# Hybrid decoder step on one core: new order of the attention and linear units, inverse roots on GpSimd, residual additions on VectorE

## The chip, the core and the metric

One program runs on one core of a Trainium2 chip. The time is the device time of a whole execution in microseconds. Lower is better. The engines are TensorE (PE, with its weight loads PEld), VectorE (DVE), ScalarE (ACT), GpSimd (POOL) and the DMA queues, of which the one on SyncE (SP) brings the weights and the one on GpSimd brings the cache. Each engine works through its own list in order, and semaphores join the lists.

## The reference

The kernel computes one inference step of a two-layer trunk for a prompt of 512 tokens and 8 samples with a paged past of 4096 tokens. Layer 0 is differential attention beside gated linear attention, layer 1 a recurrent block, and each layer ends in an MLP. What the change touches is this:

```python
def rmsnorm(x, g):
    xf = x.astype(jnp.float32)
    y = xf * lax.rsqrt(jnp.mean(xf * xf, axis=-1, keepdims=True) + EPS)
    return (y * g.astype(jnp.float32)).astype(x.dtype)
...
    a_out = rmsnorm(attend(da_q, da_k, da_v), g_da) * (1.0 - lam_init)      # diff_probs = softmax(l1) - lam * softmax(l2)
...
    def step(S, inp):                                                       # a chunk of 16 tokens
        o = jnp.einsum('bchs,bshv->bchv', att, vc) + jnp.einsum('bchk,bhkv->bchv', qe, S)
        S = jnp.exp(b_last)[..., None] * S + jnp.einsum('bshk,bshv->bhkv', kd, vc)
...
    o = rmsnorm(o.astype(h.dtype), g_gla) * jax.nn.silu(g_og)
...
        yp = yp + rmsnorm(mp, g[1])                                         # and again behind the MLP, g[3]
```

## The kernel before

All activations lie in transposed tiles of 128 features by 520 tokens (512 of the prompt, 8 samples). Weights stream in chunks of 1 MB; ScalarE splits each into a high part and VectorE into a low part, and TensorE makes three products (line 1689). This fills the long stages at the start and behind 613 us.

Between lies the mixer of layer 0. It interleaves two kinds of work:

- **The cache of the samples.** 128 pieces of 1 MB (64 of K, 64 of V) pass through a ring of 6 buffers. GpSimd issues each load (line 672) when the piece 6 places ahead has been used. Of each K piece GpSimd multiplies one half (line 629) and VectorE the other (1225), and VectorE reduces both (1213 for GpSimd's half, 1227 for its own). The function `k_chunks` does one K piece: reduce GpSimd's half of the piece before, then its own half of this one. GpSimd's next product waits for that first reduction, since it writes the same tile. V pieces are multiplied on TensorE (1850) with weights that GpSimd copies into `PM` (642).
- **The prompt.** First 16 attention units (4 heads by 4 query blocks), whose length in keys is 128, 256, 384, 512 in turn. Per unit: scores (1837), bias and row maximum on VectorE (1381, 1384, `maxima`), exponentials on ScalarE (868, `exponents`), inverse sums (1410), two scaled identities `DG` on ScalarE (915, 916), transposed difference of both softmaxes on TensorE (1878, 1879), its copy `AT` (923), and the output (1890). Then 8 linear units (4 blocks of 128 tokens by 2 head pairs). Per unit: transpose and mask the keys (1907, `KDM` 951), scores (1913), 8 updates on TensorE in two halves of 4 (1923), the chain of 8 states on VectorE (1449, `ST`), output products (1937, 1946), a state update for one sample (1827 and 1370), and three K and three V pieces.

Each unit's output is normalised two steps later: clamp (1390, 1393), sum of squares (904, `NSQ`), root on ScalarE (906, `NRT`), reciprocal and overflow test on VectorE (1399, 1400, `NRS`), a scaled identity (890, `NDG`), a product (1865) and a copy back (896).

The residual stream `X` has 8 tiles. Four times a norm of `ACC` is added to it (`post`): VectorE scales two tiles into `TMP` (1193) and adds the even one (1196), GpSimd adds the odd one (679). In the first and third of these VectorE also makes `H_lo` (1186) between the pairs.

The order on each engine is written out by hand; no scheduler moves anything. The unit loops before, on ScalarE (lines 908 to 928) and on VectorE (1406 to 1420), begin so:

```python
            if u + 1 < len(UNITS):
                exponents(u + 1)
            act.wait_ge(rr_ready, u + 1)
            A(DG[:, 0], IDENT, ACT.Copy, scale=RR[:, u % 2, 0:1])
...
            if u + 1 < len(UNITS):
                maxima(u + 1)
            ve.wait_ge(ex_done, u + 1)
            V.reciprocal(RR[:, u % 2], SM[:, u % 2]).then_inc(rr_ready, 1)
```

## Time and profile before

| | us |
|---|---|
| median of 3 runs | 1708.78 (1707.37 to 1712.07) |
| the profiled execution | 1708.17 |
| its span, first to last instruction | 1706.4 |
| attention units with cache work | about 237 to 393 |
| linear units with cache work | about 408 to 590 |
| the four residual additions | 676, 1074, 1284 and 1681 to 1694 |

The page's slices (one tenth of busy share per digit, 42.7 us each) show what kind of stage each is: TensorE stands at 9 in the long products and between 4 and 7 in the ten slices from 213 us on, which hold the units; the granted clock stands between 5 and 8 tenths there. A stage's own limits are read from the chain of waits and from the busy times of a window.

### The profile page before, as it was taken

Reading aid. Unit: us, or ns where it says so; the run is one execution under the profiler, and the core shown is the slowest. Engines: PE = TensorE matmul, PEld = TensorE weight load, DVE = VectorE, ACT = ScalarE, POOL = GpSimd, SP = SyncE. Lnnn points to the kernel's source line nnn. Section 1 sums busy time; section 2 is a strip of 40 time slices with the busy share of each in tenths; the row PEclk is TensorE's granted clock in tenths of the full one; section 3 lists DMA queues with packets and bytes.
Section 4 is the critical chain, followed back from the end, with each engine's and each line's share of the span. In section 5 each row is a group of like instructions: output and inputs, shape, how many; then the busy total and the mean of one; then the engine's idle time right before and its main releaser. Section 6 shows DMA issues by size and latency. Waiting matters only on the chain.

```text
span 1706.4 us, 25826 instructions
## 1 busy us (share of the span) xinstructions
PE 1462.3 (86%) x11004; PEld 1303.1 (76%) x11004; DVE 923.4 (54%) x1164; ACT 554.8 (33%) x861; POOL 346.4 (20%) x238
## 2 busy tenths in 40 slices
PE   4999946666667777999999999699897999999994
PEld 3999813334323366899999999589886999999994
DVE  3498867665777443743434352767718434343533
ACT  3323346662333323322222122437333222121222
POOL 0176755553555200100000000100302000000001
PEclk8999968887566679999999999799999999999997
DMA  8377688786767832123322322022221222223211
GB/s 289 124 270 258 250 288 325 294 315 257 287 229 274 295 142 75 60 90 100 99 75 99 99 78 97 3 74 76 75 75 49 79 96 99 87 87 99 89 61 51
DMA packets 127892, 250.32 MB, mean 147 GB/s; under 512 B 5267, under 2 KB 108455, under 8 KB 111136
## 3 DMA queue, kind: packets, MB, share of 16 engines
q0 software_dynamic: 18432, 134.23, 20.9%
q1 hardware_dynamic: 101984, 105.00, 19.2%
q10 hardware_dynamic: 7368, 9.50, 1.8%
q8 instruction: 87, 1.43, 0.4%
q14 instruction: 21, 0.17, 0.0%
HBM read 241.04 MB, written 7.73 MB: 146 GB/s over the span
## 4 chain that ended last, share of the span: by engine, by line
PE 74%; DVE 13%; ACT 7%; POOL 2%; issue 2%; DMA 1%; ACTq 0%; POOLq 0%; DVEq 0%
PE PS L1689 60%; PE PS L1674 3%; PE PS L1850 2%; POOL PROD L629 2%; DVE TMP L1193 2%; DVE SC L1213 1%; DVE RS L1167 1%; ACT PR L868 1%; PE PS L1923 1%; PE PS L1865 1%; PE PS L1983 1%; PE PS L1890 1%; PE PS L1878 1%; DVE PR L1381 1%; DVE MX L1384 1%
## 5 line engine op out<-in xcount | busy, mean ns | idle before, releaser
L1689 PE MATMUL PS<-H_hi,W_hi 128*128 128x260 f32 x1936 | 397.7, 287 | 24.7 <-DVE H_lo L1163 13.2
L1689 PE MATMUL PS<-H_hi,W_lo 128*128 128x260 f32 x1936 | 393.8, 285 | 0.0
L1689 PE MATMUL PS<-H_lo,W_hi 128*128 128x260 f32 x1936 | 393.6, 285 | 0.0
L1689 PEld LDWEIGHTS PS<-H_hi,W_hi 128*128 128x128 f32 x1936 | 303.8, 191 | 29.3 <-issue 22.1
L1689 PEld LDWEIGHTS PS<-H_hi,W_lo 128*128 128x128 f32 x1936 | 302.7, 191 | 0.0
L1689 PEld LDWEIGHTS PS<-H_lo,W_hi 128*128 128x128 f32 x1936 | 302.4, 191 | 0.0
L1158 DVE TENSOR_TENSOR W_lo<-RAW,W_hi 128x2048 fp32r<-128x2048 f32 x94 | 217.4, 2312 | 130.3 <-ACT W_hi L754 129.6
L754 ACT ACTIVATE W_hi<-RAW 128x2048 fp32r<-128x2048 f32 x94 | 179.4, 1909 | 278.0 <-PE PS L1689 277.7
L679 POOL TENSOR_TENSOR X<-X,TMP 128x520 f32<-128x520 f32 x16 | 26.7, 1668 | 938.8 <-DVE TMP L1193 938.8
L1689 PE MATMUL PS<-U_hi,W_lo 128*128 128x260 f32 x1024 | 206.4, 283 | 0.0
L1689 PE MATMUL PS<-U_lo,W_hi 128*128 128x260 f32 x1024 | 206.0, 283 | 0.0
L1689 PE MATMUL PS<-U_hi,W_hi 128*128 128x260 f32 x1024 | 206.0, 282 | 0.0
L629 POOL TENSOR_TENSOR PROD<-KV,QB 128x1024 f32<-128x1024 f32 x64 | 152.1, 2376 | 193.5 <-DVE SC L1213 164.4
L1689 PEld LDWEIGHTS PS<-U_hi,W_hi 128*128 128x128 f32 x1024 | 157.9, 188 | 0.0
L1689 PEld LDWEIGHTS PS<-U_hi,W_lo 128*128 128x128 f32 x1024 | 157.9, 188 | 0.0
L1689 PEld LDWEIGHTS PS<-U_lo,W_hi 128*128 128x128 f32 x1024 | 157.4, 188 | 0.0
L1553 DVE TENSOR_TENSOR ACC<-ACC,PS 128x520 f32<-128x520 f32 x64 | 44.6, 697 | 200.3 <-PE PS L1689 200.3
L1017 ACT ACTIVATE UF<-SQ 128x520 f32<-128x520 f32 x64 | 40.8, 638 | 279.9 <-DVE SQ L1543 279.9
L1850 PE MATMUL PS<-KV,PM 128*32 128x512 f32 x512 | 89.0, 782 | 29.8 <-POOL PM L642 20.7
L1543 DVE SCALAR_TENSOR_TENSOR SQ<-PS,RS 128x520 f32<-128x520 f32 x64 | 44.8, 700 | 112.9 <-PE PS L1689 112.9
L1674 PE MATMUL PS<-SQ,ONES 128*128 128x260 f32 x256 | 74.8, 449 | 36.0 <-ACT SQ L776 36.0
L1674 PEld LDWEIGHTS PS<-SQ,ONES 128*128 128x128 f32 x256 | 53.2, 222 | 56.8 <-issue 28.7
(292 smaller groups left out, 1598.7 us busy)
## 6 DMA issues: line engine op xcount, KB each, us to landing
RAW<-in_w_up SPq DMA_DIRECT2D x32, 1024.0 KB
RAW<-in_w_down SPq DMA_DIRECT2D x32, 1024.0 KB
RAW<-in_w_in_even SPq DMA_DIRECT2D x13, 1024.0 KB
RAW<-in_w_in_odd SPq DMA_DIRECT2D x8, 1024.0 KB
RAW<-in_w_out_odd SPq DMA_DIRECT2D x5, 1024.0 KB
RAW<-in_w_out_even SPq DMA_DIRECT2D x4, 1024.0 KB
x_saved<-X ACTq DMA_DIRECT2D x1, 2080.0 KB, 6.4
X<-x_saved SPq DMA_DIRECT2D x1, 2080.0 KB, 10.0
```

Source lines behind the costliest of these rows:

```text
L629: nc.gpsimd.tensor_tensor(PROD[:, 1], KV[i % RING][:, 2:4, :], QB[:, None, b % 2, :].to_broadcast([P, 2, 512]), ALU.mult).then_inc(prod1_r ...
L679: nc.gpsimd.tensor_tensor(X[:, kt], X[:, kt], TMP[:, 1], ALU.add).then_inc(x_odd, 1)
L754: A(W_hi[:, ch.slot], RAW[:, ch.slot], ACT.Copy).then_inc(w_hi_ready, 1)
L868: t = A(PR[:, u % 2, c, 0:n], PR[:, u % 2, c, 0:n], ACT.Exp, bias=MX[:, u % 2, c:c + 1], accum_out=SM[:, u % 2, c:c + 1])
L1017: A(UF[:, i], RL[:, i], ACT.Square).then_inc(uf_ready, 1)
L1158: V.tensor_tensor(W_lo[:, ch.slot], RAW[:, ch.slot], W_hi[:, ch.slot].bitcast(F32), ALU.subtract).then_inc(w_lo_ready, 1)
L1193: t = V.scalar_tensor_tensor(TMP[:, q], ACC[:, kt + q], VEC[:, gain + kt + q:gain + kt + q + 1], RS[:, 1], ALU.mult, ALU.mult)
L1543: V.scalar_tensor_tensor(pair(RL[:, i]), banks(ch.par[i]), 0.0, pair(RS[:, 1]), ALU.max, ALU.mult).then_inc(banks_free[ch.par[i]], 1)
L1553: V.tensor_tensor(pair(ACC[:, m]), pair(ACC[:, m]), banks(ch.par[i]), ALU.add).then_inc(banks_free[ch.par[i]], 1)
L1674: t = MM_(PS[:, 4 + i, 0:HALF], ONES[:], SQ[:, kt % 2, half], start=kt == 0, stop=kt == KT - 1)
L1689: t = MM_(PS[:, 2 * ch.par[i] + j, 0:HALF], w[:, ch.slot, k, cols], x[:, k, half], start=k == 0 and n == 0, stop=k == KT - 1 and n == 2)
L1850: t = MM_(PS[32 * pos:32 * pos + 32, 4, :], PM[:, part % 2, at:at + 32], KV[i % RING][:, pos, :], start=n % 32 == 0, stop=n % 32 == 31)
```

## The change

Seven edits, all in hand-written order or in who does an operation:

1. Attention, ScalarE: `DG` of a unit comes ahead of the exponentials of the next, and the copy `AT` ahead of the squares, `NDG` and the decay powers.
2. Attention, VectorE: the inverse sums of a unit come ahead of the maxima of the next.
3. The root on ScalarE and the reciprocal on VectorE go. GpSimd computes mean plus epsilon (one `tensor_scalar`) and raises it to the power -0.5 (one `tensor_tensor`), for 1 or 2 numbers per partition; the tables put this behind certain V pieces or ahead of certain K products. The overflow test stays on VectorE.
4. Linear units, TensorE: the second half of the updates has space of its own (banks 0 to 2), so it follows the first half at once; the state values come ahead of the normalisation; the normalisation and its copy stand ahead of the outputs, and the outputs wait once for all 8 states.
5. Linear units, VectorE: the second K piece and the overflow test come behind the state chain instead of ahead.
6. Linear units, ScalarE: `silu` stands ahead of the copy of the normalised output instead of behind.
7. VectorE adds all 8 residual tiles; the zeroing of `ACC` stays on GpSimd.

```diff
@@ gpsimd
+        POWERS_BEFORE_K = {K_IN_UNITS: (14, 15), **{K_IN_UNITS + 3 * u + 2: (15 + u,) for u in range(1, 6)}}
+        POWER_BEHIND_V = {**{2 * u + 1: u - 1 for u in range(1, 15)}, 51: 21, 54: 22, 57: 23}
+        def power(u):
+            n = len(outputs(u))
+            po.wait_ge(squares_summed, u + 1)
+            nc.gpsimd.tensor_scalar(NRT[:, u % 2, 0:n], NSQ[:, u % 2, 0:n], 2.0 ** -9, EPS / 1024, ALU.mult, ALU.add).then_inc(power_base, 1)
+            po.wait_ge(power_base, u + 1)
+            if u >= 2:
+                po.wait_ge(nd_ready, outputs_done(u - 1))
+            nc.gpsimd.tensor_tensor(NRS[:, u % 2, 0:n], NRT[:, u % 2, 0:n], EPSC[:, 2:2 + n], ALU.pow).then_inc(root_done, 1)
...
-        def post_add(i):
-            for kt in range(1, KT, 2):
-                po.wait_ge(post_odd, 4 * i + kt // 2 + 1)
-                nc.gpsimd.tensor_tensor(X[:, kt], X[:, kt], TMP[:, 1], ALU.add).then_inc(x_odd, 1)
@@ scalar, attention units
-            if u + 1 < len(UNITS):
-                exponents(u + 1)
             act.wait_ge(rr_ready, u + 1)
             A(DG[:, 0], IDENT, ACT.Copy, scale=RR[:, u % 2, 0:1])
             A(DG[:, 1], IDENTL[:], ACT.Copy, scale=RR[:, u % 2, 1:2]).then_inc(dg_ready, 1)
+            if u + 1 < len(UNITS):
+                exponents(u + 1)
+            act.wait_ge(at_done, u + 1)
+            A(AT[:, 0:n], PS[:, 2, 0:n], ACT.Copy).then_inc(at_copied, 1)
...
@@ vector
-                ve.wait_ge(post_even, 4 * i + kt // 2 + 1)
-                V.tensor_tensor(X[:, kt], X[:, kt], TMP[:, 0], ALU.add).then_inc(x_even, 1)
+                for q in range(2):
+                    ve.wait_ge(post_scaled, 8 * i + kt + q + 1)
+                    V.tensor_tensor(X[:, kt + q], X[:, kt + q], TMP[:, q], ALU.add).then_inc(x_added, 1)
...
@@ tensor, linear units
+            if u:
+                pe.wait_ge(st_ready, 8 * u)
             for first in (0, 4):
-                if first or u:
-                    pe.wait_ge(st_ready, 8 * u + first)
+                if first:
+                    pe.wait_ge(attm_ready, 2 * u + 2)
                 for n in range(first, first + 4):
...
-            if u:
-                normalise(15 + u, 2)
             state_values(u)
+            pe.wait_ge(st_ready, 8 * u + 8)
             v_chunks(34 + 3 * u, 1)
+            if u:
+                normalise(15 + u)
+                pe.wait_ge(nev_done, outputs_done(16 + u))
```

How the instructions stand, in the program's own lists. A bracket names the semaphores that an instruction waits for. ScalarE in the attention unit of head 2, first query block, before (its next unit has 256 keys):

```order
L868 ACTIVATE PR,SM<-PR,MX 128x256 [waits nm_ready]
L868 ACTIVATE PR,SM<-PR,MX 128x256
L915 ACTIVATE DG<-CONST,RR 128x128 [waits rr_ready]
L916 ACTIVATE DG<-IDENTL,RR 128x128
L904 ACTIVATE SQJ,NSQ<-OTC 128x128 [waits clamped]
L906 ACT_TABLE_LOAD
L906 ACTIVATE NRT<-NSQ,EPSC 128x1 [waits act_step]
L890 ACTIVATE NDG<-CONST,NRS 128x128 [waits nr_ready]
L923 ACTIVATE AT<-PS 128x128 [waits at_done]
L896 ACTIVATE PJ<-PS,G_129 128x128 [waits nmm_done]
L927 ACTIVATE OT<-PS 128x128 [waits o_done]
L868 ACT_TABLE_LOAD
```

and now:

```order
L926 ACTIVATE DG<-CONST,RR 128x128 [waits rr_ready]
L927 ACTIVATE DG<-IDENTL,RR 128x128
L883 ACTIVATE PR,SM<-PR,MX 128x256 [waits nm_ready]
L883 ACTIVATE PR,SM<-PR,MX 128x256
L931 ACTIVATE AT<-PS 128x128 [waits at_done]
L918 ACTIVATE SQJ,NSQ<-OTC 128x128 [waits clamped]
L905 ACTIVATE NDG<-CONST,NRS 128x128 [waits nr_ready]
L911 ACTIVATE PJ<-PS,G_129 128x128 [waits nmm_done]
L940 ACTIVATE OT<-PS 128x128 [waits o_done]
```

`DG` has moved ahead of the exponentials `PR`, `AT` ahead of the squares, and of the two table loads of a unit and the root none is left.

GpSimd in the fourth linear unit (K products `PROD`, cache loads `DMA`, weights of V pieces `PM`), before:

```order
L629 TENSOR_TENSOR PROD<-KV_69,QB 128x1024 [waits prod1_used,kv_loaded0]
L642 COPY PM<-SC_79 128x16x8 [waits soft_done,v_used]
L672 DMA KV_70<-in_cache_v,CIDX 128x2048 [waits v_used]
L672 DMA KV_69<-in_cache_k,CIDX 128x2048 [waits prod1_ready,k_used]
L629 TENSOR_TENSOR PROD<-KV_69,QB 128x1024 [waits prod1_used,kv_loaded2]
L672 DMA KV_69<-in_cache_v,CIDX 128x2048 [waits v_used]
L672 DMA KV_69<-in_cache_k,CIDX 128x2048 [waits prod1_ready,k_used]
```

and now:

```order
L638 TENSOR_TENSOR PROD<-KV_69,QB 128x1024 [waits prod1_used,kv_loaded0]
L651 COPY PM<-SC_79 128x16x8 [waits soft_done,v_used]
L699 DMA KV_70<-in_cache_v,CIDX 128x2048 [waits v_used]
L699 DMA KV_69<-in_cache_k,CIDX 128x2048 [waits prod1_ready,k_used]
L662 TENSOR_SCALAR NRT<-NSQ 128x2 [waits squares_summed]
L666 TENSOR_TENSOR NRS<-NRT,EPSC 128x2 [waits nd_ready,power_base]
L638 TENSOR_TENSOR PROD<-KV_69,QB 128x1024 [waits prod1_used,kv_loaded2]
L699 DMA KV_69<-in_cache_v,CIDX 128x2048 [waits v_used]
L699 DMA KV_69<-in_cache_k,CIDX 128x2048 [waits prod1_ready,k_used]
```

The two instructions of the power stand behind the second K product of the unit and the two loads that follow it, ahead of the third.

VectorE in the same linear unit, before (`SC` and `PROD` are a K piece, `S_163` the state of a sample):

```order
L1441 COPY_PREDICATED ATTM<-CONST,PS 128x128 [waits go_done,att_done,dve_step]
L1441 COPY_PREDICATED ATTM<-CONST,PS 128x128 [waits go_done,att_done]
L1213 TENSOR_REDUCE SC_74<-PROD 128x2x8 [waits prod1_ready]
L1225 TENSOR_TENSOR PROD<-KV_69,PS 128x1024 [waits kv_loaded0]
L1227 TENSOR_REDUCE SC_74<-PROD 128x2x8 [waits k_used]
L1399 RECIPROCAL NRS<-NRT 128x2 [waits root_done,dve_step]
L1400 SCALAR_TENSOR_TENSOR NRS<-NSQ,NRS 128x2 [waits dve_step]
L1449 SCALAR_TENSOR_TENSOR ST<-ST,DECC,PS 128x128 [waits u_done]
L1449 SCALAR_TENSOR_TENSOR ST<-ST,DECC,PS 128x128 [waits st_ready] x3
L1449 SCALAR_TENSOR_TENSOR ST<-ST,DECC,PS 128x128 [waits u_done,st_ready]
L1449 SCALAR_TENSOR_TENSOR ST<-ST,DECC,PS 128x128 [waits st_ready] x3
L1370 SCALAR_TENSOR_TENSOR S_163<-PS,KSS,S_163 64x128 [waits gs_v_done,st_ready]
```

and now:

```order
L1456 COPY_PREDICATED ATTM<-CONST,PS 128x128 [waits go_done,att_done,dve_step]
L1456 COPY_PREDICATED ATTM<-CONST,PS 128x128 [waits go_done,att_done]
L1461 SCALAR_TENSOR_TENSOR ST<-ST,DECC,PS 128x128 [waits u_done]
L1461 SCALAR_TENSOR_TENSOR ST<-ST,DECC,PS 128x128 [waits st_ready] x3
L1461 SCALAR_TENSOR_TENSOR ST<-ST,DECC,PS 128x128 [waits u_done,st_ready]
L1461 SCALAR_TENSOR_TENSOR ST<-ST,DECC,PS 128x128 [waits st_ready] x3
L1229 TENSOR_REDUCE SC_74<-PROD 128x2x8 [waits prod1_ready,st_ready]
L1241 TENSOR_TENSOR PROD<-KV_69,PS 128x1024 [waits kv_loaded0]
L1243 TENSOR_REDUCE SC_74<-PROD 128x2x8 [waits k_used]
L1415 SCALAR_TENSOR_TENSOR NRS<-NSQ,NRS 128x2 [waits root_done,dve_step]
L1386 SCALAR_TENSOR_TENSOR S_163<-PS,KSS,S_163 64x128 [waits gs_v_done]
L1386 SCALAR_TENSOR_TENSOR S_163<-PS,KSS,S_163 64x128 x3
```

The second K piece has moved behind the 8 states; the overflow test `NRS` waits there for `root_done`, which GpSimd now gives, and the state of the sample and the third K piece stand behind it.

## Rows read from the trace of the kernel before

**Rows 1.** The page: the span.
```profile
span 1706.4 us, 25826 instructions
```

**Rows 2.** Windows of attention and linear units: length, busy us (instructions), clock, DMA.
```profile
237.00:393.00 156.00, 105.41 (x590) 53.27 (x590) 101.28 (x164) 94.39 (x229) 88.65 (x71) 0.85 0.82 310
408.00:590.00 182.00, 123.04 (x843) 60.61 (x847) 126.72 (x213) 59.01 (x169) 92.82 (x72) 0.63 0.70 261
```

**Rows 3.** TensorE's timeline, outputs of first and last attention unit: start, us.
```profile
243.53 0.49 PE L1890 MATMUL PS<-VT,AT 128*128 128x128 f32 x2
...
391.05 1.16 PE L1890 MATMUL PS<-VT,AT 128*128 128x128 f32 x8 [0.46 <-ACT PJ L896]
```

**Rows 4.** Chain of waits through one attention unit (512 keys next): start, us.
```profile
334.43 1.08 PE PS L1837 x4
...
338.05 1.52 ACT PR L868 x4
...
345.00 0.74 PE PS L1865 x2
...
345.77 0.38 ACT PJ L896
346.19 0.82 PE PS L1890 x5
```

**Rows 5.** ScalarE's groups: table loads at the root; count, busy us, mean ns.
```profile
L906 ACT ACT_TABLE_LOAD x20 | 25.7, 1283 | 0.3
```

**Rows 6.** VectorE's timeline in the same unit: overflow test and one K piece.
```profile
338.38 0.16 DVE L1400 SCALAR_TENSOR_TENSOR NRS<-NSQ,NRS 128x1 f32<-128x1 f32 x1
338.46 1.22 DVE L1213 TENSOR_REDUCE SC<-PROD 128x16 f32<-128x1024 f32 x1
339.58 1.21 DVE L1225 TENSOR_TENSOR PROD<-KV,PS 128x1024 f32<-128x1024 f32 x1
```

**Rows 7.** GpSimd's timeline: a K product, a load, a small copy.
```profile
339.82 2.36 POOL L629 TENSOR_TENSOR PROD<-KV,QB 128x1024 f32<-128x1024 f32 x1 [3.64 <-DVE SC L1213]
...
344.47 0.94 POOL L672 DMA_INDIRECT KV<-in_cache_k,CIDX  x1 [0.30 <-issue]
...
355.02 0.40 POOL L642 COPY PM<-SC 128x128 f32<-128x128 f32 x1
```

**Rows 8.** Window of the attention stage in which DMA is fullest.
```profile
360.00:370.00 10.00, 5.58 (x36) 2.79 (x37) 6.66 (x12) 7.79 (x21) 3.34 (x5) 0.99 0.99 408
```

**Rows 9.** Cache tiles in the attention stage, issue to landing.
```profile
DMA to landing us min/median/max: 5.2/8.0/10.6
```

**Rows 10.** VectorE's timeline in the fourth linear unit, from clamp to clamp.
```profile
481.89 0.42 DVE L1393 TENSOR_SCALAR OTC<-PS 128x256 f32<-128x256 f32 x1 [6.39 <-ACT OT L963]
...
493.78 1.50 DVE L1449 SCALAR_TENSOR_TENSOR ST<-ST,DECC,PS 128x128 f32<-128x128 f32 x4 [1.65 <-PE PS L1923]
497.78 1.45 DVE L1370 SCALAR_TENSOR_TENSOR S<-PS,KSS,S 64x128 f32<-64x128 f32 x4 [2.50 <-PE PS L1827]
...
504.22 0.41 DVE L1393 TENSOR_SCALAR OTC<-PS 128x256 f32<-128x256 f32 x1
```

**Rows 11.** TensorE's timeline: outputs of that unit, then the next unit's transpose.
```profile
499.47 0.80 PE L1937 MATMUL PS<-GVT,ATTM 128*128 128x128 f32 x2
...
502.98 0.47 PE L1907 MATMUL PS<-CONST,KD 128*128 128x128 f32 x1
```

**Rows 12.** Timeline of the second residual addition, VectorE and GpSimd.
```profile
1074.45 1.43 DVE L1193 SCALAR_TENSOR_TENSOR TMP<-ACC,VEC,RS 128x520 f32<-128x520 f32 x2
1075.80 0.69 DVE L1196 TENSOR_TENSOR X<-X,TMP 128x520 f32<-128x520 f32 x1
1075.96 1.67 POOL L679 TENSOR_TENSOR X<-X,TMP 128x520 f32<-128x520 f32 x1 [381.55 <-DVE TMP L1193]
...
1076.53 2.34 DVE L1193 SCALAR_TENSOR_TENSOR TMP<-ACC,VEC,RS 128x520 f32<-128x520 f32 x2
...
1079.51 2.34 DVE L1193 SCALAR_TENSOR_TENSOR TMP<-ACC,VEC,RS 128x520 f32<-128x520 f32 x2
```

More of the change, by code:

```diff
@@ L230, in trunk @@
     V_CONVW, V_CONVB, V_BA, V_BX, V_LAM = 64, 96, 104, 112, 120
-    EPSC = small("EPSC", 2)
+    EPSC = small("EPSC", 4)
     PTB = sb("PTB", [P, N_SAMPLE * N_PAGES], I32, r_1 + 33792)
@@ L533, in outputs_done, with update, norm_bank @@
         return u if u <= len(UNITS) else 2 * u - len(UNITS)
+    def update(n, rows):
+        bank, at = (3, n) if n < 4 else (n // 2 - 2, 2 + n % 2)
+        return PS[rows, bank, P * at:P * at + P]
+    def norm_bank(u, i):
+        return PS[:, 3, P:2 * P] if u < len(UNITS) else PS[:, i, 2 * P:3 * P]
     def state(tb, n):
@@ L643, in weights @@
                                   SC[b % SLOTS][:, :, 16 * half:16 * half + 16].rearrange("p j n -> p n j")).then_inc(pm_ready, 1)
+        K_IN_UNITS = sum(UNIT_STEPS) + 2 * 11 + sum(PRE_STEPS)
+        POWERS_BEFORE_K = {K_IN_UNITS: (14, 15), **{K_IN_UNITS + 3 * u + 2: (15 + u,) for u in range(1, 6)}}
[8 more added lines that the diff above has]
+            nc.gpsimd.tensor_tensor(NRS[:, u % 2, 0:n], NRT[:, u % 2, 0:n], EPSC[:, 2:2 + n], ALU.pow).then_inc(root_done, 1)
         def release(i):
@@ L657, in release @@
                 po.wait_ge(v_used, n + 1)
+                if n in POWER_BEHIND_V:
+                    power(POWER_BEHIND_V[n])
         AHEAD = 1
@@ L664, in _ @@
                     if j < LOADS and ORDER[j][0] == "k":
+                        for u in POWERS_BEFORE_K.get(ORDER[j][1], ()):
+                            power(u)
                         pool_product(ORDER[j][1])
@@ L901, in squares_of @@
             act.wait_ge(clamped, u + 1)
-            n = len(outputs(u))
             for i, (at, tile, cols) in enumerate(outputs(u)):
                 t = A(SQJ[:, at], OTC[:, at], ACT.Square, scale=2.0 ** -4, accum_out=NSQ[:, u % 2, i:i + 1])
-            link(t)
-            A(NRT[:, u % 2, 0:n], NSQ[:, u % 2, 0:n], ACT.Sqrt, scale=2.0 ** -9, bias=EPSC[:, 1:2]).then_inc(root_done, 1)
+            t.then_inc(squares_summed, 1)
         act.wait_ge(identl_ready, 1)
@@ L1398, in inverse_norm @@
             n = len(outputs(u))
-            link(V.reciprocal(NRS[:, u % 2, 0:n], NRT[:, u % 2, 0:n]))
             V.scalar_tensor_tensor(NRS[:, u % 2, 0:n], NSQ[:, u % 2, 0:n], SQUARE_OVERFLOWS ** 2 / 256, NRS[:, u % 2, 0:n],
@@ L1406, in _ @@
         for u in range(len(UNITS)):
+            ve.wait_ge(ex_done, u + 1)
+            V.reciprocal(RR[:, u % 2], SM[:, u % 2]).then_inc(rr_ready, 1)
             if u + 1 < len(UNITS):
                 maxima(u + 1)
-            ve.wait_ge(ex_done, u + 1)
-            V.reciprocal(RR[:, u % 2], SM[:, u % 2]).then_inc(rr_ready, 1)
             if u:
@@ L1859, in past_output, with normalise @@
             t.then_inc(ogt_done, 1)
-        def normalise(u, bank):
+        def normalise(u):
             for i, (at, tile, cols) in enumerate(outputs(u)):
                 pe.wait_ge(nd_ready, outputs_done(u) + i + 1)
-                MM_(PS[:, bank, P + P * i:2 * P + P * i], OT[:, at], NDG[:, at], start=True, stop=True).then_inc(nmm_done, 1)
+                MM_(norm_bank(u, i), OT[:, at], NDG[:, at], start=True, stop=True).then_inc(nmm_done, 1)
         scores(0)
```

77 lines of the change are left out of this document (32 added, 45 removed).

## The prediction

> **What bounds the kernel now.** I read the span first [rows 1], then the windows of the two loops of units, then the chain of waits through one unit, then what each engine does there. The profiled execution took 1708.17 us, 1.8 us more than its span, and lies 0.6 us under the median of the three runs, so a sum made against it holds for the median as well. TensorE is full outside the mixer. Inside it no engine is: in the attention stage TensorE is busy 105 of 156 us, VectorE 101, ScalarE 94, GpSimd 89, and DMA 82% [rows 2]. What sets the end there is a chain that goes round all of them. Row by row in the unit shown: scores 1.08, VectorE's bias and maxima, exponentials 1.52, `DG`, then the transposes, a V piece, the normalisation 0.74, its copy 0.38, the output, and only then the next scores [rows 4]. From the first unit's output to the last one's it is 391.05 - 243.53 = 147.5 us, 9.8 us for each of 15 units [rows 3]. The linear stage takes 182 us with VectorE busy 127 of them [rows 2]; one unit is 22.3 us from clamp to clamp, and VectorE waits for TensorE twice in it, 1.65 and 2.50 us [rows 10]. The four residual additions are short chains in which TensorE only sums.
>
> **Attention units (edits 1, 2 and 3).** `DG` of a unit no longer waits for the maxima and exponentials of the next, so TensorE's transposes and first V piece run beside them. The new loop through ScalarE is: scores, maxima, exponentials, `AT`, squares, `NDG`, normalisation, its copy, output. In the unit shown: 5.1 up to the exponentials [rows 4], about 0.5 + 0.5 + 0.4 for the three on ScalarE (the like of the copy there, 0.38, with hand-overs), 0.74 + 0.38, output 0.9: 8.5 us. By the same count the other three lengths give 7.1, 5.8 and 7.1 (the parts in front shrink with the keys), 7.1 in the mean. The table loads cost 1.28 us each [rows 5]; the program has 54 before and 17 now, 37 fewer or 47 us of ScalarE, but ScalarE wasn't full, and only those on this loop count; they are already out of it in the sum. The Trainium skill says in "ScalarE: Activation LUTs", section on table sets, that a change of set costs about 2.7 us and that work should be batched by set. The trace agrees with the batching and disagrees with the price, 1.28 against 2.7; by the page's figure the removed loads would be 100 us of ScalarE and not 47.
>
> Two other limits stand close to it. One is DMA: a unit brings 3 pieces, 3.15 MB, and the fullest window moved 408 GB/s at 99% [rows 8]: 7.7 us per unit. The other is new. GpSimd now does the power of a unit behind its second V piece, and VectorE waits for it ahead of its K piece, whose first reduction GpSimd's next product waits for. Round that loop: overflow test 0.16, reduction 1.22 [rows 6], hand-over 0.1, product 2.36, two loads with their gaps 2.5 [rows 7], 0.2 for the copy into `PM` that falls on every second unit, hand-overs 0.3, and the power: 6.9 us plus x.
>
> **The price of a power, x.** The trace shows no power. It is two dependent GpSimd instructions on 1 or 2 numbers per partition. The nearest row is the copy of 128 numbers per partition, 0.40 us; the farthest is the product of 1024 at 2.36 us [rows 7]. So a pair lies between 0.2 us (two instructions of half the small copy) and 4.7 us (two of the large). I take two small copies and a hand-over, 0.9 us, since one number is much nearer to 128 than to 1024. Then GpSimd's loop is 7.8 us. The Trainium skill's "GPSIMD Engine Reference", section on instruction dispatch, says that the first call of a freshly loaded GpSimd kernel costs about 6 us more; no row here shows such a call, and if a power needed one the sum would be about 6 us worse, once.
>
> With limits of 7.1, 7.7 and 7.8 us that don't peak in the same units, and with 0.5 to 1.5 us of preparation of the linear units on VectorE in eight of the units, I take 8.5 us. 15 x (9.8 - 8.5) = 20 us saved. The floor is 7.8 (30 saved), and the ceiling, if the cache pieces land late, is 9.8 (nothing). VectorE's reciprocal (0.15) is gone too, and hidden.
>
> At the hand-over to the linear units the powers 14 and 15 stand in GpSimd's list ahead of the first K product and behind two loads, and the copy and squares of unit 15 wait for the first of them. Before, VectorE had the root in hand at once. I charge 2.5 us (the two loads) on the path to the sample's state outputs.
>
> **Linear units (edits 3 to 6).** The two waits of 1.65 and 2.50 us go: the second half of the updates follows at once, and the state values are ready early. But the second K piece, which stood ahead of the states while TensorE worked, now stands behind them, and behind it VectorE waits for the power. GpSimd can start its product only when the first reduction of that K piece is done, then issues two loads, then does the power: 0.1 + 2.36 + 2.5 + 0.9 = 5.9 us later [rows 7], while VectorE needs only 2.4 for the rest of the K piece [rows 6]. It stands 3.4 us. Behind it are the state of the sample (1.45) and the third K piece on VectorE, and `NDG`, the product, its copy and the outputs (3.5 us [rows 11]) on the way to the clamp. From the end of the states: K piece 3.65, wait 3.4, test 0.2, then `NDG` 0.7, product 1.2, `silu` with its table load or the copy 1.3 to 1.9, outputs 3.5, copy and clamp 0.7 (the small ones by the like of rows 4, with hand-overs), together about 15; from the clamp to the end of the states 8.4 (V piece 1.9, two halves of updates 4.0, the rest). 23.5 us against 22.3 [rows 10]. The first unit, where the K piece filled a wait, loses 2.7; the middle five lose about 1 each, the last two nothing. I take +8 us, with bounds -10 (both old waits gained, no new one) and +20 (x of 2.5 us).
>
> The last normalisation now waits for a power that GpSimd does after a V piece is used, on the way to the output projection: x, the test, `NDG` and hand-overs, +2.2 us.
>
> **Residual additions (edit 7).** Before, each pair after the first has one scaling held up by GpSimd's addition: two scalings take 2.34 us where undisturbed they take 1.43, and from pair to pair it is 2.98 us [rows 12]. With GpSimd out and one more addition of 0.69 on VectorE a pair is 1.35 + 0.65 + 0.70 = 2.70. Three pairs save 0.8, and at the end VectorE's last addition is done 0.5 us earlier than GpSimd's. The two with `H_lo` come to 1.2 in the same way, since there one `H_lo` was held up. 4 x 1.25 = 5 us saved, all on the path, since TensorE waits for the sums.
>
> **Sum.** -20 + 2.5 + 8 + 2.2 - 5 = -12.3 us, 1708.2 - 12.3 = 1696 us.
>
> **Rivals.** (a) The linear units gain too. If GpSimd's loads and product run ahead so that the power waits for nobody, VectorE's two waits are simply gone: 8 units x 2.5 us or so less than I count, some 14 us. 1682 us. For it: GpSimd is idle half of this stage (93 of 182 us [rows 2]). Against it: the power's place behind the second product.
>
> (b) The attention units are held by the cache. The ring reaches two units ahead. Loads go out after the product, some 8 us into a unit, and land 8.0 us later at the median, 10.6 at most [rows 9]; two units of 8.5 leave only 1.5 us beyond the median. If DMA near its full rate lands later, the period settles at 9.3 us: 12 us less gain, 1708 us, no change.
>
> (c) Slower: the power is dear. GpSimd's two instructions at 1.2 us and more each hold 15 attention units (period 6.9 + x), 7 linear units and the two hand-overs. From x = 1.6 on each further microsecond costs 24. The sum reaches zero near x = 1.8; at x = 2.2 the time is 1717 us. For it: this operation is the only one here with no row. Against it: it has one number per partition.
>
> **Chances.** Forecast 0.42, with its own range 1688 to 1702; (a) 0.20; (b) 0.15; (c) 0.15; the remaining 0.08 is linear units that lose much more than I count, 1704 to 1712. One measurement tells about 0.3% from no change, 5 us, so faster means under 1703.6 and slower over 1713.9. Faster takes the forecast, (a) and a fifth of (b) and little more: 0.66. Same takes most of (b) and some of the rest: 0.14. Slower takes (c), a fifth of (b) and the worst of the rest: 0.20. The range 1677 to 1714 leaves out most of (c) and the best of (a).
>
> **What would show it.** In the profile after: period of the attention outputs (8.5 us); span between GpSimd's `NRT` and `NRS` starts and the next load (0.9 us); VectorE's idle time ahead of `NRS` in units 1 to 5 of the linear part (3.4 us, put down to GpSimd); clamp to clamp 23.5 us; pairs of additions 2.70 us. I am wrong if the attention period stays over 9.3 us, if the power pair takes over 1.6 us, or if VectorE doesn't wait ahead of the overflow test in the linear units.

## The result and the profile after

The changed kernel takes 1682.07 us (median of 4 runs, 1680.55 to 1683.37) against 1709.13 us: ratio 0.984, interval 0.9823 to 0.9857, 27 us faster. The forecast was 1696 us, 13 us faster. The sign and the range held; the size was about half of what came. The profiled execution of the changed kernel took 1682.64 us, and its page says

```profile
span 1680.8 us, 25820 instructions
```

which is 25.6 us less than [rows 1]. The windows of the two loops of units in the changed kernel (length, busy us of PE, PEld, DVE, ACT and POOL, clock, DMA share, GB/s) answer to [rows 2]:

```profile
242.00:364.00 122.00, 97.36 (x568) 46.92 (x560) 96.79 (x143) 54.72 (x184) 95.11 (x93) 0.86 0.95 365
386.00:565.00 179.00, 117.37 (x831) 59.54 (x831) 121.13 (x210) 44.09 (x148) 98.60 (x84) 0.64 0.71 258
```

From first to last output the attention stage is a sixth shorter with the same work: DMA went from 82% to 95%, ScalarE fell from 94 of 156 us to 55 of 122. TensorE's first and last attention outputs answer to [rows 3]:

```profile
242.42 0.49 PE L1904 MATMUL PS<-VT,AT 128*128 128x128 f32 x2
...
365.37 0.82 PE L1904 MATMUL PS<-VT,AT 128*128 128x128 f32 x5 [0.46 <-ACT PJ L911]
```

365.37 - 242.42 = 123.0 us, 8.2 us a unit instead of 9.8. Between such landmarks both executions can be laid side by side. OS is VectorE's first operation on the sample's state outputs. The clamps are those of [rows 10], one for each linear unit; the linear units are numbered 0 to 7, and "unit 3" is the time from the clamp of [rows 10] to the next. The output projection is its first product, line 1704 now.

| stretch | before | after | change | forecast |
|---|---|---|---|---|
| start to first attention output | 243.5 | 242.4 | -1.1 | |
| first to last attention output | 147.5 | 123.0 | -24.6 | -20 |
| last output to OS (hand-over) | 16.4 | 20.5 | +4.1 | +2.5 |
| OS to first clamp (linear unit 0) | 20.2 | 23.0 | +2.8 | +2.7 |
| first to eighth clamp | 158.0 | 155.8 | -2.2 | +5 |
| eighth clamp to output projection | 27.3 | 29.9 | +2.6 | +2.2 |
| the rest, with the four additions | 1093.4 | 1086.2 | -7.2 | -5 |

In linear unit 3 (clamp to clamp, VectorE; start, us, what, and in brackets the idle time ahead and its releaser) the rows answer to [rows 10]:

```profile
459.90 0.42 DVE L1409 TENSOR_SCALAR OTC<-PS 128x256 f32<-128x256 f32 x1 [6.84 <-ACT OT L977]
...
464.61 3.03 DVE L1461 SCALAR_TENSOR_TENSOR ST<-ST,DECC,PS 128x128 f32<-128x128 f32 x8 [0.25 <-PE PS L1939]
467.67 1.22 DVE L1229 TENSOR_REDUCE SC<-PROD 128x16 f32<-128x1024 f32 x1
468.81 1.21 DVE L1241 TENSOR_TENSOR PROD<-KV,PS 128x1024 f32<-128x1024 f32 x1
470.05 1.22 DVE L1243 TENSOR_REDUCE SC<-PROD 128x16 f32<-128x1024 f32 x1
475.33 0.16 DVE L1415 SCALAR_TENSOR_TENSOR NRS<-NSQ,NRS 128x2 f32<-128x2 f32 x1 [4.06 <-POOL NRS L666]
475.41 1.43 DVE L1386 SCALAR_TENSOR_TENSOR S<-PS,KSS,S 64x128 f32<-64x128 f32 x4
...
481.90 0.42 DVE L1409 TENSOR_SCALAR OTC<-PS 128x256 f32<-128x256 f32 x1
```

The two waits of [rows 10] are gone in this unit: the 8 states now run in one piece, and the sample's state waits no longer for TensorE. In their place stands 4.06 us for `NRS`, which GpSimd gives. GpSimd's timeline in the same unit shows what stood ahead of it:

```profile
469.04 2.36 POOL L638 TENSOR_TENSOR PROD<-KV,QB 128x1024 f32<-128x1024 f32 x1 [2.69 <-DVE SC L1229]
...
471.89 1.01 POOL L699 DMA_INDIRECT KV<-in_cache_v,CIDX  x1 [0.16 <-issue]
...
474.22 0.19 POOL L662 TENSOR_SCALAR NRT<-NSQ 128x2 f32<-128x2 f32 x1
474.50 0.72 POOL L666 TENSOR_TENSOR NRS<-NRT,EPSC 128x2 f32<-128x2 f32 x1
```

The product starts when VectorE has done the first reduction of the K piece behind the states. Then come the copy of the V weights, two loads and the power. The two instructions of a power take 0.19 + 0.72 us for two numbers per partition, 1.0 us from start to end, and 0.8 for one number. VectorE stands 3.7 to 4.6 us for the power in units 2 to 5, but only 1.15 us in unit 1 (at 423.00 us) and 2.2 us in unit 6.

### The profile page after: what moved, and what is told of

It reads as the page before. It is cut to its first block, busy times and chain, and to the rows that moved or that the text cites. A ratio compares the mean times of both kernels' runs of the same rounds, so it can differ in the third digit from the quotient of the medians.

```text
span 1680.8 us, 25820 instructions
## 1 busy us (share of the span) xinstructions
PE 1455.7 (87%) x11004; PEld 1298.4 (77%) x11004; DVE 913.1 (54%) x1157; ACT 500.1 (30%) x800; POOL 339.4 (20%) x270
## 3 DMA queue, kind: packets, MB, share of 16 engines
q8 instruction: 87, 1.43, 0.3%
## 4 chain that ended last, share of the span: by engine, by line
PE 74%; DVE 13%; ACT 4%; POOL 4%; issue 2%; DMA 2%; ACTq 0%; DVEq 0%; POOLq 0%
PE PS L1704 61%; PE PS L1689 3%; POOL PROD L638 3%; PE PS L1864 2%; DVE SC L1229 2%; DVE RS L1182 1%; PE PS L1939 1%; DVE TMP L1208 1%; PE PS L1996 1%; POOL KV L699 1%; DVE ST L1461 1%; DVE X L1212 1%; DVE ACC L1613 1%; PE PS L1959 1%; DMA out_gla_prompt<-ST 1%
## 5 line engine op out<-in xcount | busy, mean ns | idle before, releaser
L715 POOL TENSOR_TENSOR INP<-GX,ACC 128x520 f32<-128x520 f32 x7 | 14.5, 2079 | 505.9 <-ACT GX L1100 499.4
```

## The experiments

Each starts from the changed kernel unless it says otherwise. "Attention" is first to last attention output, "linear" OS to the eighth clamp, in the profiled execution.

| kernel | median us | ratio to before, interval | attention | hand-over | linear |
|---|---|---|---|---|---|
| before | 1707.6 to 1714.2 | | 147.5 | 16.4 | 178.2 |
| the changed kernel | 1682.07 | 0.984 [0.9823, 0.9857] | 123.0 | 20.5 | 178.8 |
| e1 linear power early | 1672.39 | 0.9789 [0.9767, 0.9811] | 123.1 | 19.3 | 169.6 |
| e2 linear root on ScalarE | 1670.37 | 0.9772 [0.9745, 0.98] | 122.9 | 19.2 | 169.3 |
| e3 attention order back | 1701.33 | 0.9958 [0.9939, 0.9977] | 144.5 | 18.2 | 180.9 |
| e4 additions back | 1690.5 | 0.9884 [0.986, 0.9908] | 123.4 | 20.4 | 181.5 |
| e5 attention root on ScalarE | 1708.91 | 0.9992 [0.9976, 1.0009] | 149.8 | 16.0 | 180.4 |
| e6 power longer | 1707.57 | 0.9984 [0.9968, 0.9999] | 132.5 | 22.7 | 192.2 |
| e7 e1 and copy early | 1662.82 | 0.9725 [0.9697, 0.9753] | 122.9 | 20.5 | 160.6 |
| e8 copy early alone | 1675.45 | 0.9788 [0.9759, 0.9817] | 124.1 | 20.4 | 174.2 |
| e9 half the bytes of V | 1684.41 | 0.9848 [0.981, 0.9885] | 123.0 | 19.2 | 179.9 |
| e10 all powers early | 1653.04 | 0.9673 [0.9641, 0.9705] | 124.2 | 15.3 | 158.1 |
| e11 e10, copies early everywhere | 1651.94 | 0.9663 [0.9629, 0.9698] | 123.2 | 17.1 | 154.1 |
| e12 K piece ahead | 1666.44 | 0.9752 [0.9722, 0.9781] | 123.4 | 19.3 | 161.0 |
| e13 e12, halves share space | 1675.65 | 0.9771 [0.9742, 0.98] | 123.6 | 20.8 | 179.1 |
| e14 silu behind | 1685.95 | 0.9835 [0.981, 0.9859] | 123.1 | 20.8 | 181.4 |
| e15 e11, K piece ahead | 1647.35 | 0.9622 [0.9594, 0.965] | 123.1 | 15.9 | 151.6 |
| e16 e15, linear root on ScalarE | 1654.86 | 0.9656 [0.9628, 0.9685] | 122.7 | 17.5 | 154.4 |

The kernel before was measured again beside each group of experiments, and its median moved between 1707.6 and 1714.2 us; where two groups are compared, the ratios are the better guide. The last three columns come from one execution each. Kernels that share the program of a stage show how far such a column wanders: 122.9 to 124.1 us in attention, 19.2 to 20.8 at the hand-over, and 178.8 to 181.5 in the linear units (the changed kernel, e3, e4, e5 and e9). A difference inside these bands says nothing.

**Attention: which edit?**

```diff
@@ e3: scalar (vector likewise: maxima(u + 1) ahead of the inverse sums)
+            if u + 1 < len(UNITS):
+                exponents(u + 1)
             act.wait_ge(rr_ready, u + 1)
             A(DG[:, 0], ...)                       # and AT again behind decay_powers
@@ e5: scalar, squares_of(u), u < 16 (e2 further down: the same for u >= 16)
+                link(t)
+                A(NRT[...], NSQ[...], ACT.Sqrt, ...).then_inc(root_done, 1)     # reciprocal on VectorE
```

> The changed kernel with ScalarE's and VectorE's order in the attention units put back (exponentials and maxima of the next unit ahead of the scaled identities and inverse sums, the copy AT behind the squares), the power kept on GpSimd. The attention outputs lie 8.2 us apart in the changed kernel and 9.8 us in the one before. Theory (the order made the gain, the root's table loads only little): period 9.3 us or more, time 1698 us or more. Rival (the 2 table loads of 1.28 us per unit that went made it): period 8.6 us or less, time under 1689 us.

> The changed kernel with the roots of the 16 attention units back on ScalarE (square root, reciprocal on VectorE), the new order kept; the linear units keep the power. Theory (the two edits need each other: in the new loop the squares stand between the copy AT and the normalisation, so a root puts its two table loads of 1.28 us on the loop through ScalarE, while in the old order they cost only 3 us in all): attention period 9.3 us or more against 8.2, time 1697 us or more. Rival (the order alone gives the gain, the cache's transfers hold the period near 8.2 us anyway): period 8.5 us or less, time under 1688 us.

The numbers of both theories came out (periods of 9.6 and 10.0 us). The reason that e3's theory gave, that the order alone made the gain, did not; e5's, that the edits need each other, did. With neither edit the stage takes 147.5 us, with the power alone 144.5, with the order alone 149.8, with both 123.0: the first is worth 3 us alone, the second nothing, together they are worth 24.6. TensorE's timeline of e3 (the transposes of two units in a row) shows why the power alone gives little: they still wait for `DG`, which stands behind the next unit's exponentials.

```profile
311.12 0.49 PE L1892 MATMUL PS<-DG,PR 128*128 128x128 f32 x2 [2.28 <-ACT DG L929]
...
321.23 0.49 PE L1892 MATMUL PS<-DG,PR 128*128 128x128 f32 x2 [2.33 <-ACT DG L929]
```

ScalarE's timeline of e5 shows why the order alone gives nothing: between `AT` and the normalised copy (at 317.07) stand the squares, the table load, the root, `NDG`, a second load, and the decay powers `KD`, the exponential that needs it.

```profile
312.01 0.60 ACT L942 ACTIVATE AT<-PS 128x512 f32<-128x512 f32 x1 [2.57 <-PE PS L1906]
...
312.91 1.28 ACT L928 ACT_TABLE_LOAD   x1
314.20 0.29 ACT L928 ACTIVATE NRT<-NSQ,EPSC 128x1 f32<-128x1 f32 x1
314.41 0.39 ACT L912 ACTIVATE NDG<-CONST,NRS 128x128 f32<-128x128 f32 x1
314.81 1.28 ACT L906 ACT_TABLE_LOAD   x1
316.10 1.06 ACT L906 ACTIVATE KD<-KD 128x1024 f32<-128x1024 f32 x1
```

**Attention: what holds the 8.2 us?**

```diff
@@ e9: gpsimd, loads
+                if kind == "v" and 6 <= n < 32:
+                    dst, src = dst[:, 0:1024], ...  # half a row
@@ e6: gpsimd, power(u)
+            for k in range(2):
+                po.wait_ge(power_base, 3 * u + 1 + k)
+                nc.gpsimd.tensor_tensor(NRX[:, 0:n], NRT[:, u % 2, 0:n], EPSC[:, 2:2 + n], ALU.pow).then_inc(power_base, 1)
```

> The changed kernel, but the loads of V pieces 6 to 31 (those of the attention units) bring only half of the bytes (half of each row, from other rows of the cache), so an attention unit brings 2.1 MB instead of 3.15 MB; GpSimd issues as many loads, and the output of the past's attention is not the reference's. Theory A (transfers set the 8.2 us between attention outputs, with DMA at 95% and 365 GB/s there): first to last attention output 117 us or less instead of 123.0, time 1677 us or less. Theory B (the loops through the engines, GpSimd's of 7.8 us and ScalarE's, set it): 121 us or more, time 1680 to 1683 us.

> The changed kernel with two more powers ahead of each power, into a spare tile, so that the pair of GpSimd instructions of 0.85 us becomes about 2.2 us long. Theory A (GpSimd's loop of K product, loads and power is the next limit in attention, at 7.8 us): period 9.0 to 9.2 us instead of 8.2, and with the linear units, the two hand-overs and the end 20 us or more: 1702 us or more. Theory B (the cache's transfers set the 8.2 us and the power stands beside them): period under 8.5 us, the rest of the program 6 to 10 us, time 1688 to 1693 us.

The transfers don't hold it. The window of the attention stage, of the changed kernel and then of e9:

```profile
237.00:365.00 128.00, 102.35 (x582) 48.58 (x582) 97.79 (x144) 55.06 (x186) 97.36 (x96) 0.85 0.92 354
```

```profile
237.00:365.00 128.00, 102.10 (x582) 50.42 (x582) 98.71 (x145) 54.91 (x185) 97.35 (x97) 0.85 0.73 255
```

354 GB/s become 255 and DMA falls from 92% to 73%, and the first and last attention outputs stay 123.0 us apart, as theory B said. (The median, 1684.41 us, lies 1.4 us over its range; the ratio is that of the changed kernel within the interval.) In e6 the pair is longer by 1.5 us in the linear units (GpSimd's timeline, the two extra powers and the real one):

```profile
495.53 1.49 POOL L666 TENSOR_TENSOR NRX<-NRT,EPSC 128x2 f32<-128x2 f32 x2
497.10 0.69 POOL L670 TENSOR_TENSOR NRS<-NRT,EPSC 128x2 f32<-128x2 f32 x1
```

and by 1.3 in attention. The attention stage grew by 9.5 us, 0.6 a unit, to a period of 8.8 us. Neither theory's period holds (9.0 to 9.2, or under 8.5), though theory A's time of 1702 us or more does. A reading that fits is that GpSimd's loop is the longest in part of the units only. The whole kernel lost 25.5 us, most of the rest (13.4) in the linear units. GpSimd's loop in the changed kernel reads

```profile
316.73 1.84 POOL L699 DMA_INDIRECT KV<-in_cache_v,CIDX  x1 [0.15 <-POOL PROD L638]
318.88 0.94 POOL L699 DMA_INDIRECT KV<-in_cache_k,CIDX  x1 [0.30 <-issue]
319.89 0.19 POOL L662 TENSOR_SCALAR NRT<-NSQ 128x1 f32<-128x1 f32 x1
320.16 0.56 POOL L666 TENSOR_TENSOR NRS<-NRT,EPSC 128x1 f32<-128x1 f32 x1
320.90 1.01 POOL L699 DMA_INDIRECT KV<-in_cache_v,CIDX  x1 [0.18 <-issue]
323.17 2.34 POOL L638 TENSOR_TENSOR PROD<-KV,QB 128x1024 f32<-128x1024 f32 x1 [1.26 <-DVE SC L1229]
325.68 1.85 POOL L699 DMA_INDIRECT KV<-in_cache_v,CIDX  x1 [0.16 <-POOL PROD L638]
```

Where GpSimd's loop holds a unit (it stands idle only 0.3 us ahead of its product), one turn is 7.1 us when both issues behind the product are short (products at 290.25 and 297.38), and 8.0 us when one of them takes 1.85 us, as in the rows above (products at 323.17 and 331.15; in e9 at 314.31, 322.28 and 330.25).

**The linear units: the power's place, and who stands beside it.**

```diff
@@ e1: gpsimd
-        ... **{K_IN_UNITS + 3 * u + 2: (15 + u,) for u in range(1, 6)}}
+        ... **{K_IN_UNITS + 3 * u + 1: (15 + u,) for u in range(1, 6)}}
@@ e7 (with e1), e8 (alone): gpsimd, ahead of the products of a step
+                if ORDER[i - RING][0] == "v" and ORDER[i - RING][1] >= 32:
+                    next_weights(ORDER[i - RING][1])          # the copy into PM
```

> The changed kernel with one edit: in linear units 1 to 5 the power stands ahead of the second K product instead of behind it and its two loads. In the changed kernel VectorE stands 3.7 to 4.6 us ahead of the overflow test in each of these units. Theory: this wait is on the path and nothing else is close behind it, so clamp to clamp of these five units falls from 22-25 us to 18-19 us and the time from 1682 to about 1663 us. Rival: another limit (the cache pieces' landing, TensorE's third V piece, GpSimd's own products) is right behind; then the wait goes but clamp to clamp stays over 20.5 us and the time over 1674 us.

> The changed kernel with the roots of the 8 linear units back on ScalarE (square root, reciprocal on VectorE), all orders kept. Theory (the power's place behind GpSimd's product costs the linear units 3.7 to 4.6 us each, and the root itself was never on the path there, since ScalarE idles 13 us in a unit): the wait of VectorE goes, its two table loads per unit are hidden, time 1660 to 1668 us. Rival (the root off ScalarE is what paid for the linear units): the table loads come on the path between the normalisation and the outputs, 1680 us or more.

> The first experiment (power of linear units 1 to 5 ahead of the second K product) and besides, in the linear units, the copy of the V weights (PM) ahead of the K product instead of behind it. In the first experiment units 3 and 4 fell from 22 to 18-20 us, unit 5 stayed at 25 us and unit 2 at 26.5, where a V piece waits for that copy. Theory (in these units a second chain of about the same length, product, copy, V piece, stands beside VectorE's wait for the power): unit 5 falls to 20-21 us, unit 2 by 2 to 3 us, time 1664 to 1667 us. Rival (something else holds these units): 1670 us or more.

> The changed kernel with only the copy of the V weights moved ahead of the K product in the linear units, the power where it is. Theory (two chains side by side, the wait for the power being the longer or equal): unit 5 stays within 1.5 us of 25, in all at most 4 us faster than the changed kernel, 1678 to 1682 us; the sum of this and of the first experiment's gain is smaller than the gain of both together. Rival (the copy was the limit and the power's wait beside it costs nothing): unit 5 at 21 us, time under 1677 us.

e1 lies between its two numbers. Its expectation says that VectorE waits 3.7 to 4.6 us in each of units 1 to 5; that holds for units 2 to 5. Units 3 and 4 fell from 22.0 and 22.4 us to 18.2 and 19.7, but unit 5 stayed at 25.1 and unit 2 at 26.5. VectorE's timeline of e1: in unit 4 the test waits for nothing; in unit 5 neither, but the sample's state behind it waits 4.38 us for TensorE.

```profile
485.91 0.16 DVE L1415 SCALAR_TENSOR_TENSOR NRS<-NSQ,NRS 128x2 f32<-128x2 f32 x1
...
506.34 0.16 DVE L1415 SCALAR_TENSOR_TENSOR NRS<-NSQ,NRS 128x2 f32<-128x2 f32 x1
510.88 1.45 DVE L1386 SCALAR_TENSOR_TENSOR S<-PS,KSS,S 64x128 f32<-64x128 f32 x4 [4.38 <-PE PS L1841]
...
518.63 0.42 DVE L1409 TENSOR_SCALAR OTC<-PS 128x256 f32<-128x256 f32 x1 [2.22 <-ACT OT L977]
```

The chain of waits there goes through GpSimd's product, the copy into `PM`, and the V piece that needs it:

```profile
504.07 2.35 POOL PROD L638
506.42 0.35 POOL PM L651
...
506.90 1.94 PE PS L1864 x8
508.84 2.00 PE PS L1841 x2
510.84 1.86 PE PS L1864 x8
```

e7 moves this copy ahead too, and unit 5 falls to 18.8 us: the time is 1662.8 us, just under the theory's range. e8, the copy alone, gave 6.6 us: its time lies on the rival's side, since unit 2 fell from 28.2 to 24.0, where the copy alone was last; unit 5 fell to 23.6, within the theory's 1.5 us. The gains are 9.7 and 6.6 us alone and 19.3 together (8.7, 8.9 and 19.7 by the ratios); the 2 to 3 us between sum and whole are no more than the intervals allow. Unit 5 is the clear sign of two chains side by side: 25.0 us, 25.1 with the power early, 23.6 with the copy early, 18.8 with both. e2, just outside its first range, takes the linear units to 169.3 us, as e1 does: they lose 9 us by the power's place.

**The linear units: the K piece, the two halves, silu.**

```diff
@@ e12: vector, linear units
             slot(GLA_SLOT + 2 * u)
+            k_chunks(min(max(steps - 1, 0), 1))
             for n in range(8):
...
-            k_chunks(min(max(steps - 1, 0), 1))
@@ e13 (with e12): tensor
+        return PS[rows, 3, P * (n % 4):P * (n % 4) + P]
+                if first or u:
+                    pe.wait_ge(st_ready, 8 * u + first)
@@ e14: scalar
             if u:
                 normalised(15 + u)
+            if 1 <= u <= 4:
+                A(PJ[:, 19 + u], PJ[:, 19 + u], ACT.Silu).then_inc(silu_ready, 1)
```

> The changed kernel with the second K piece of the linear units ahead of the 8 states on VectorE again, as in the kernel before; the overflow test stays behind the states. Theory (with the K piece behind, GpSimd's product starts late, and the power behind it is what VectorE and TensorE wait for; with it ahead the product runs beside the states): the wait for the power falls from 4 us to under 1.5 us, units 1 to 5 at 19 to 21 us, 1668 to 1674 us. Rival (the states come 3.7 us later and TensorE's outputs with them, which eats it): 1680 us or more.

> The experiment with the K piece ahead of the states, and in it the two halves of the updates share space again, so that the second half waits for the first 4 states (with the V piece between the halves, as before). Theory (this edit alone is what the linear units gain most by, since VectorE's wait between the two halves, 1.65 to 2.15 us in every unit before, is on the path in all 8 units): 1.5 to 2.5 us per unit given back, first clamp to last 152 to 158 us instead of 141.9, time 1677 to 1684 us. Rival (the gain comes from the outputs' and the state values' place instead): under 5 us in all, time under 1672 us.

> The changed kernel with silu behind the copies of the normalised output again on ScalarE (units 1 to 4). I had charged silu 1.3 to 1.9 us on the path of each unit in its new place; in the trace of the changed kernel it takes 0.62 us beside the product. Theory (silu is off the path in both places, no table load is left there): within 2 us of the changed kernel, 1680 to 1684 us. Rival (its place decides when the outputs start): 1685 us or more.

e12 is 15.6 us faster than the changed kernel, more than expected, though units 1 and 2 stay at 24.5 and 24.8 us. VectorE's timeline, unit 3: the K piece fills the time of the updates, GpSimd's product runs beside the states, and the wait for the power is 1.73 us instead of 4.06 (under 1.5 was expected).

```profile
460.11 1.22 DVE L1229 TENSOR_REDUCE SC<-PROD 128x16 f32<-128x1024 f32 x1
...
463.75 3.03 DVE L1462 SCALAR_TENSOR_TENSOR ST<-ST,DECC,PS 128x128 f32<-128x128 f32 x8
468.51 0.16 DVE L1415 SCALAR_TENSOR_TENSOR NRS<-NSQ,NRS 128x2 f32<-128x2 f32 x1 [1.73 <-POOL NRS L666]
```

e13 takes back the halves' own space and loses 9.2 us by the medians, 3 us by the ratios, whose intervals overlap; its time lies between its theory and its rival. Its profiled execution was the slowest of its four and shows 18.1 us more in the linear units. So the own space probably gains, but the ratios don't show it clear of noise, and how much stays open; the place of the state values and outputs was not tested by itself. e14 is 3.9 us slower than the changed kernel by the medians, which is the rival's side, but 0.0005 apart by the ratios (the kernel before was 0.3% slower beside it): no difference is shown.

**The additions.**

```diff
@@ e4: gpsimd
+                nc.gpsimd.tensor_tensor(X[:, kt], X[:, kt], TMP[:, 1], ALU.add)
```

> The changed kernel with the odd residual tiles added by GpSimd again, and nothing else. Theory: the four additions give 7.2 us, as the starts of the stages in the two traces say, so 1689.3 us, and the pair of additions takes 2.98 us again. Rival: what I had counted, 5 us or less, the rest being from elsewhere: 1687 us or less.

8.4 us slower (7.5 by the ratios), 7.9 of them in the stretch that holds the additions, near the theory's 7.2. VectorE's timeline of the changed kernel in the last one:

```profile
1658.18 1.43 DVE L1208 SCALAR_TENSOR_TENSOR TMP<-ACC,VEC,RS 128x520 f32<-128x520 f32 x2
1659.53 1.30 DVE L1212 TENSOR_TENSOR X<-X,TMP 128x520 f32<-128x520 f32 x2
1660.75 1.42 DVE L1208 SCALAR_TENSOR_TENSOR TMP<-ACC,VEC,RS 128x520 f32<-128x520 f32 x2
```

A pair is 1660.75 - 1658.18 = 2.57 us; in e4 it is 2.98 again. The whole addition takes 10.3 us (1658.18 to 1668.52) instead of 12.1 (1681.76 to 1693.86 in the kernel before): 1.8 us each, 7 us for four.

**What the experiments point to.**

```diff
@@ e10 (with e7); e11: the copies of the attention units too
-        POWERS_BEFORE_K = {K_IN_UNITS: (14, 15), ...
+        POWERS_BEFORE_K = {K_IN_UNITS - 1: (14,), K_IN_UNITS: (15,), ...
-        POWER_BEHIND_V = {..., 51: 21, 54: 22, 57: 23}
+        POWER_BEHIND_V = {..., 50: 21, 53: 22, 56: 23}
@@ e15: e11 with e12's order; e16: e15 with e2's roots
```

> The experiment with the power and the copy ahead of the K product, and besides power 14 ahead of the K product of the last attention unit, and powers 21 to 23 behind the V piece before. Theory (the hand-over to the linear units, 20.5 us against 16.4 before, and unit 6 with 22 us wait for a power in GpSimd's list): hand-over 17 us, unit 6 at 19 to 20 us, the end 1 us less, 1655 to 1658 us. Rival (the squares of unit 14 come too late, or the power now holds back GpSimd's product): 1661 us or more.

> As the last one, with the copy of the V weights ahead of the K product in the attention units too. Theory (in the attention units a loop of GpSimd with the copy in every second unit is close to the limit, but transfers and TensorE stand beside it): 0 to 4 us faster than the last one. Rival (the copy holds the K product back by 0.4 us in every second unit): 0 to 4 us slower.

> The kernel with all powers and all copies early (1652 us), and the K piece of the linear units ahead of the states as well. Theory (with the power early, VectorE waits for nothing behind the states, and the K piece ahead only fills what is left of its wait for TensorE's updates, under 1.4 us per unit): 0 to 8 us faster, 1644 to 1652 us. Rival (the states come 3.7 us later and TensorE's outputs with them): 1655 us or more.

> The last one with the roots of the 8 linear units on ScalarE instead of GpSimd. Theory (the power has a place there where nobody waits for it, so it makes no difference who does it): within 3 us of the last one. Rival (taking it off GpSimd frees GpSimd's loop): 4 us or more faster.

e10 is 9.8 us faster than e7 and better than its range, with the hand-over at 15.3 us and the way to the output projection at 25.1 instead of 29.9. e11 is the same within its interval. e15, at 1647.35 us, is the fastest: 3.8% under the kernel before. In its unit 3 VectorE waits for nothing from the K piece behind one clamp to the next clamp, 17.6 us on:

```profile
441.78 0.42 DVE L1417 TENSOR_SCALAR OTC<-PS 128x256 f32<-128x256 f32 x1 [3.73 <-ACT OT L985]
...
449.78 3.03 DVE L1470 SCALAR_TENSOR_TENSOR ST<-ST,DECC,PS 128x128 f32<-128x128 f32 x8
452.85 0.16 DVE L1423 SCALAR_TENSOR_TENSOR NRS<-NSQ,NRS 128x2 f32<-128x2 f32 x1
452.93 1.44 DVE L1394 SCALAR_TENSOR_TENSOR S<-PS,KSS,S 64x128 f32<-64x128 f32 x4
...
459.37 0.41 DVE L1417 TENSOR_SCALAR OTC<-PS 128x256 f32<-128x256 f32 x1
```

e16 came out as neither its theory nor its rival: with the power in a place where nobody waits for it, the roots on ScalarE look 7.5 us dearer, 0.3% by the ratios, whose intervals overlap; a small loss is likely and not shown. In the changed kernel the same roots had saved 12 us. So it was the power's place that those 12 us came from, not the root itself.

## Why the prediction was right in its sign and short in its size

The profiled executions give -25.6 us where the sum gave -12.3. By terms:

- **Attention, 5.7 us short** (-25.7 with the start, against -20; the start's 1.1 us is inside what that stretch varies, 241.9 to 244.8 us in kernels with the same attention program). The mechanism held: `DG` off the next unit's exponentials, roots off ScalarE's loop, GpSimd's loop next. The loops were counted as 7.1, 7.7 and 7.8 us, and GpSimd's came out at 7.1, or 8.0 with a long issue. I then put 0.7 us on top for limits that don't peak together and chose 8.5; 8.2 came. The limit from the transfers, 7.7 us, was no limit (e9). What the text lacked is that the two edits are worth almost nothing apart. It wrote the 37 table loads off as hidden; e5 has 27 of them back with the attention roots, and its attention stage is 27 us longer.
- **The hand-over, 1.6 us too good**: +4.1 against +2.5, or +2.8 to +4.4 by the band of this stretch. The power of attention unit 14 stood behind a product and two loads, and e10, which moves it ahead, gives the loss back.
- **The linear units, 7.4 us short: the step that failed** ("23.5 us against 22.3 ... the middle five lose about 1 each, the last two nothing"). The new wait is there, put down to GpSimd, and about as long as said: 3.4 us forecast, 3.7 to 4.6 us measured in units 2 to 5, but 1.15 us in unit 1, which I had charged in full; unit 0 came at +2.8 against +2.7. But I counted one unit, the fourth (unit 3), at 23.5 us and charged its +1 to the five middle units. Unit 3 itself came out at 22.0: `silu` and its load, which I had on the path at 1.3 to 1.9 us, run beside the product, as ScalarE's timeline shows,

```profile
475.53 0.69 ACT L905 ACTIVATE NDG<-CONST,NRS 128x128 f32<-128x128 f32 x2 [13.06 <-DVE NRS L1415]
476.13 0.62 ACT L972 ACTIVATE PJ<-PJ 128x520 f32<-128x520 f32 x1
477.24 0.62 ACT L911 ACTIVATE PJ<-PS,G 128x128 f32<-128x128 f32 x2 [0.49 <-PE PS L1879]
```

and the updates are done 0.7 us earlier. Against before, units 1 to 7 changed by -2.3, -0.9, -0.3, +1.0, +2.4, -0.2 and -1.9 us, where +1 was forecast for five of them and nothing for the last two. (Units 1 and 2 vary by 2 us or more between executions of the same program; the others repeat to 0.8 us, but for unit 5, 23.4 us once. With the band of the whole stage the forecast is 5 to 7 us off, not exactly 7.4.) Two things were missing: the last units have the old waits too, and the gain from TensorE's edits there, which I put at nothing, is 1.9 us in unit 7; and a wait costs its length only where no other chain of the same length stands beside it, which in units 2 and 5 is the copy into `PM` (e7, e8). e12 weighs both sides: everything but the K piece's place takes the linear stage from 178.2 to 161.0 us (17 saved), and the K piece behind the states gives 17.8 back. I had 19.7 for the loss (2.7 + 5 x 3.4) and so only 12 for the gain; most of the error is this gain, 12 where 17 came.
- **The end, right**: +2.6 against +2.2.
- **Additions, 2.2 us short**: the pair is 2.57 us, not 2.70, since each of these instructions of VectorE starts 0.08 us before the last one's end (1659.53 against 1658.18 + 1.43), and I had allowed for only part of that. The stretch itself varies by 3 us between kernels that share it (1085.6 to 1088.5).

The price of a power was right (0.8 to 1.0 us against 0.9), so rival (c)'s condition did not come; its price per microsecond was nearly right: with 2.1 us a pair in attention and 2.5 in the linear units (e6) the kernel is as slow as before, where I had put the point at 1.8, and each further microsecond costs about 18 us (25.5 for 1.4), not 24. Rival (a), 1682 us, gave the right time by luck: VectorE does wait for the power. Its condition, made true for units 1 to 5 in e1, gives 1672, and with the copies and the other powers early too (e10) 1653. Its sum was also loose: 8 units x 2.5 us are 20 us and not the 14 that its time uses. Rival (b) is excluded by e9: pieces land after 6.0 us at the median instead of 8.5 there, and nothing moves; the margin of 1.5 us that it gives should by its own terms (2 x 8.5 - 8 - 8.0) be 1.0.

## What to carry to other kernels

Where work goes round several engines, count the loop with every edit of the change and without each of them: two edits that take different engines off the same loop can be worth 25 us together and 3 or nothing apart, and the price of a table load depends on the order around it. When an operation moves to another engine, its place in that engine's list can cost more than its length (here a power of 1 us, and 9 us for where it stood in five units, e1); look for what stands ahead of it. Don't multiply one unit's count: read a unit of each kind, and ask of each wait which other chain ends with it.
